# A hybrid scan-and-attention layer on one core: the low parts of the moving matrices placed 64 bytes further on

## What is computed

```python
h = adaLN(rmsnorm(x))                      # per-feature shift, scale, gate from SiLU(cond) @ w_ada
p = h @ w_in                               # q/k/v, r/k/v of the scan, low-rank codes, two branch gates
ya = rwkv_branch(...)                      # bidirectional scan with a 64x64 state per head
yb = neighbourhood_attention(...)          # 8 x 16 window of the grid, and the context tokens
x += gate1 * ((sig(gA) * (ya @ w_out_a) + sig(gB) * (yb @ w_out_b)) @ w_out)
x += gate2 * ((gelu(conv(h2 @ w_up_u)) * (h2 @ w_up_v)) @ w_ffn_down)   # h2 = adaLN(rmsnorm(x)), width 2816
```

## Time and profile before

| | |
|---|---|
| time, median of 3 runs | 2512.56 us (2512.36 to 2512.92) |
| the profiled execution's own time | 2510.91 us |
| its span, first to last instruction | 2509.1 us |
| mean granted TensorE clock | 0.983 |
| TensorE matmul busy | 2382.1 us, 95% |
| weight loads busy | 1964.0 us, 78% |
| VectorE, ScalarE, GpSimd busy | 1296.3, 725.6, 657.8 us |

### The profile page before, as it was taken

One profiled execution on the slowest core, in us unless ns is written; L12 is line 12 of the kernel. 1 busy time (PEld: TensorE's weight loads), 2 busy tenths in 40 slices (PEclk: granted clock), 3 DMA queues, 4 the chain that ended last, 5 costly groups with the idle time before them and its releaser, 6 DMA issues.

```text
span 2509.1 us, 50765 instructions
## 1 busy us (share of the span) xinstructions
PE 2382.1 (95%) x21658; PEld 1964.0 (78%) x21658; DVE 1296.3 (52%) x2077; ACT 725.6 (29%) x1189; POOL 657.8 (26%) x283
## 2 busy tenths in 40 slices
PE   5899999999999998889999998999999999999997
PEld 4777878788888887888745687888888888888886
DVE  4575657527568667895543323634333433443344
ACT  5273644634455553333300001201100110011002
POOL 2022020111211111222000244434344444444341
PEclk9999999999999999999989998999999999999999
DMA  6313111022266786676423310111111111111112
GB/s 281 109 35 106 55 60 62 28 95 76 93 193 193 202 230 191 196 204 183 154 75 115 119 35 26 34 34 43 35 42 34 43 34 43 34 42 37 40 34 93
DMA packets 224561, 234.53 MB, mean 93 GB/s; under 512 B 143922, under 2 KB 178866, under 8 KB 222898
## 3 DMA queue, kind: packets, MB, share of 16 engines
q1 hardware_dynamic: 199090, 229.55, 28.4%
q10 hardware_dynamic: 25344, 3.15, 0.8%
HBM read 173.80 MB, written 57.02 MB: 92 GB/s over the span
## 4 chain that ended last, share of the span: by engine, by line
PE 81%; DVE 8%; issue 3%; ACT 2%; DMA 2%; SPq 1%; ACTq 1%; POOL 1%; DVEq 0%; POOLq 0%
PE PS L878 20%; PE PS L879 20%; PE PS L880 20%; PE PS L1354 6%; PE PS L1022 3%; PE PS L994 2%; DVE buffer L2081 2%; PE PS L1008 1%; DVE buffer L2080 1%; PE PS L996 1%; DMA buffer<-in_w_ada_first 1%; ACTq L1729 1%; PE PS L1074 1%; PE PS L1164 1%; PE PS L1326 1%
## 5 line engine op out<-in xcount | busy, mean ns | idle before, releaser
L878 PE MATMUL PS<-buffer,buffer 128*128 128x512 f32 (+1 forms) x2784 | 997.5, 358 | 10.2 <-DVE buffer L1976 3.4
L879 PE MATMUL PS<-buffer,buffer 128*128 128x512 f32 (+1 forms) x2784 | 987.8, 355 | 1.7 <-issue 1.7
L880 PE MATMUL PS<-buffer,buffer 128*128 128x512 f32 (+1 forms) x2784 | 987.8, 355 | 0.0
L878 PEld LDWEIGHTS PS<-buffer,buffer 128*128 128x128 f32 x2784 | 525.6, 189 | 97.3 <-issue 17.0
L880 PEld LDWEIGHTS PS<-buffer,buffer 128*128 128x128 f32 x2784 | 525.6, 189 | 78.8 <-issue 2.1
L879 PEld LDWEIGHTS PS<-buffer,buffer 128*128 128x128 f32 x2784 | 525.9, 189 | 75.2 <-issue 1.0
L2366 POOL TENSOR_TENSOR buffer<-buffer,buffer 128x1024 fp32r<-128x1024 f32 x76 | 184.0, 2421 | 816.8 <-PE PS L880 510.4
L2309 DVE SCALAR_TENSOR_TENSOR buffer<-PS,buffer,buffer 128x512 f32<-128x512 f32 (+1 forms) x264 | 158.5, 655 | 151.4 <-PE PS L880 151.4
L2367 POOL TENSOR_TENSOR buffer<-buffer,buffer 128x1024 fp32r<-128x1024 f32 x76 | 194.1, 2554 | 6.0
L2285 DVE TENSOR_SCALAR buffer<-buffer,buffer 128x1281 f32<-128x1281 f32 x22 | 34.8, 1582 | 286.6 <-ACT buffer L1810 286.6
L1810 ACT ACTIVATE buffer<-PS 128x512 f32<-128x512 f32 (+1 forms) x66 | 30.0, 529 | 504.3 <-PE PS L880 504.3
(11 more groups left out here) (228 smaller groups left out, 2796.9 us busy)
## 6 DMA issues: line engine op xcount, KB each, us to landing
buffer<-in_w_up SPq DMA_DIRECT2D x44, 512.0 KB, 3.3
buffer<-in_w_in SPq DMA_DIRECT2D x42, 512.0 KB, 5.2
ops_kept<-buffer SPq DMA_DIRECT2D x40, 512.0 KB, 4.6
buffer<-ops_kept SPq DMA_DIRECT2D x80, 256.0 KB, 3.4
buffer<-in_w_ada SPq DMA_DIRECT2D x32, 512.0 KB, 6.3
buffer<-rkv_kept SPq DMA_DIRECT2D x120, 128.0 KB, 3.3
buffer<-in_w_down SPq DMA_DIRECT2D x22, 512.0 KB, 3.3
buffer<-in_x SPq DMA_DIRECT2D x20, 512.0 KB, 7.6
```

What stands on the lines that cost most here:

```text
L878: mm(out, w_hi, x_hi, start=start, stop=False)
L879: mm(out, w_hi, x_lo, start=False, stop=False)
L880: return mm(out, w_lo, x_hi, start=False, stop=stop)
```

## The change

`LO_SHIFT` of 16 words (64 bytes) is added to `LO_AT`, and so to all that is placed from it, and separately to the FFN's buffers behind `h2H`. No instruction is added, removed or moved on any engine; only addresses differ.

```diff
-        LO_AT = AFTER_YB + 12 * T
+        LO_SHIFT = 16
+        LO_AT = AFTER_YB + 12 * T + LO_SHIFT
@@
-        assert g3.at == LO_AT, (g3.at, LO_AT)
+        assert g3.at <= LO_AT, (g3.at, LO_AT)
@@
-        assert FREE + 3 * KB * T == LO_AT
+        assert FREE + 3 * KB * T <= LO_AT
@@
-        diag2 = view(FREE + 2 * KB * T, TB, P)
+        diag2 = view(FREE + 2 * KB * T + LO_SHIFT, TB, P)
@@
         h2H = view(FREE, KB, T, dtype=F32R)
-        h2_scaled_x = view(FREE + KB * T, KB, T)
-        h2L = view(FREE + KB * T, KB, T, dtype=F32R)
-        s5 = Space(FREE + 2 * KB * T)
+        h2_scaled_x = view(FREE + KB * T + LO_SHIFT, KB, T)
+        h2L = view(FREE + KB * T + LO_SHIFT, KB, T, dtype=F32R)
+        s5 = Space(FREE + 2 * KB * T + LO_SHIFT)
         factH = s5(3, T, dtype=F32R)
         factL = view(s5.at, 3, T, dtype=F32R)
```

## The result

The changed kernel takes 2532.96 us (median of 4 runs, 2530.02 to 2536.26) against 2512.46 for the kernel before: 1.0074 times as long, 95% interval 1.0056 to 1.0093. It is slower by some 20 us. The profiled execution is at 2530.02 us with a span of 2528.2, 19.1 us longer than before.

A forecast was written before the change was run, and what follows sets the result against it. The prediction took TensorE's matmuls, busy 95% of the span, to bound the kernel. Its terms summed to +0.1 us on 2510.9 profiled, 2512.6 by the median, predicted as 2512; own range 2508 to 2517, 8 in 10 range 2482 to 2537.

The forecast's parts named there:

- What bounds the kernel, and how to read it: Whole kernel: TensorE's matmuls, busy 95% of the span; only the distance between starts in an unbroken row counts.
- The sign of failure that I had named: Tiles and `ffn_up`: the forecast is wrong if distances between matmul starts change by over 1 ns on average.
- A matmul costs what its own pair of halves costs today: Split matmuls, stationary and moving operand: same half 227.2 ns wide, 119.6 narrow; different halves 229.0 and 116.4.
- `ffn_down`, which I put at -0.2 us: 528 triples of `ffn_down`: all three matmuls come to same halves; -1.9 us wide, +1.7 narrow, together -0.2.
- `tile` and `ffn_up`, -0.2: 1776 triples: only the second matmul's x moves, into its weights' half; -2.1 us wide, +1.9 narrow, together -0.2.
- the attention, 0.0: 288 triples of its projections: the first matmul gets different halves, the other two equal ones; 0.0 us.
- The bound for what I didn't know: Attention, tiles and `ffn_up`: 4128 switches of x's half, each up to 6.3 ns dearer or cheaper, +26 to -26 us; zero taken.
- The slow rival: Triples of attention, tiles and `ffn_up`: each of 4128 switches of halves costs up to 6.3 ns, +26 us, 2538.6; chance 0.26.
- The rival that nothing happens: Whole kernel: by the page's rules no placement in 64-byte steps costs anything; same time as forecast, within no change's 0.40.
- Nothing for the other engines: Moved buffers of VectorE, ScalarE and GpSimd: an engine of this kind pays nothing for the place.
- +0.5 us for `mix_block`: Plain float32 matmuls of `mix_block`: x leaves the half without their weights for theirs; 256 x 2 ns = +0.5 us.

The follow-up runs named there:

- down_only: Kernel before with only `factH` and `factL` (both together) and `x1` moved by 64 bytes; 1.0015 times the kernel before.
- ring_128_back: Kernel before with `WORDS` 32 less, so all weight tiles of the ring lie 128 bytes further back; 1.0071 times the kernel before.
- after_lo_back: Changed kernel with the ring's low weights moved 128 bytes against the high ones; 1.0037 times the kernel before, changed kernel 1.0083 on the same chip.

## Why the prediction was wrong

- **What bounds the kernel, and how to read it: right.** The sign of failure that I had named came: the distances in tiles and `ffn_up` grew by 2.6 and 3.2 ns wide. The loss is in the distance between starts in unbroken rows of split matmuls and nowhere else of size; that sum (+20.6 us) meets the measured 20.
- **"A matmul costs what its own pair of halves costs today": the step that failed.** From two placements in the trace, 0 and 192, I took a rule modulo 128. The runs show a period of 256 bytes with a sign: what I called "different halves" is 228.9 ns wide at +192 and 233.3 at +64, and "same halves" 226.9 at 0 and 232.4 at 128. So the terms had the wrong entry each time. `ffn_down`, which I put at -0.2 us as a return to the attention's state, came to a distance of 128 and cost +4.8; `tile` and `ffn_up`, -0.2, cost +12.9; the attention, 0.0, cost +3.0. Only in the attention, tiles and `ffn_up` are moving matrices mixed, and there no sum over single matmuls works either: in `ffn_up` the own distances modulo 256 give 230.1 ns of the table's 232.2, in the attention 229.0 of 233.3. The rest comes with the neighbours' operands.
- **The bound for what I didn't know: wide enough, and zero the wrong choice in it.** 4128 switches at up to 6.3 ns gave +26 us, and the wide range held that sum but for a little. So the measured 2533 us lies in it, though far outside the 2508 to 2517 of my forecast. In part that is luck: the stages that the bound was made for lost 15.9 us, and the other 4.8 are `ffn_down`'s, for which it had nothing. I chose the middle because two placements were equal within 0.2%; with an overhead that other placements move by 4 to 6 ns, equality of two of them says nothing about a third.
- **The slow rival: right in sign, near in price in part by luck, and no account of the loss.** down_only and ring_128_back lose without a switch, and after_lo_back keeps the switches and gets half of the loss back. That mixing the places of x costs something of its own is borne out, but not as a price for a switch of halves: it goes from +4.4 to -1.7 ns a matmul with the place of the weights.
- **The rival that nothing happens.** By the Trainium skill, page "SBUF — State Buffer", section "Specifications (TRN2)", the lines of SBUF have 16 bytes; taken alone, that would make every multiple of 64 bytes alike. The tables disagree for float32r: 226.9 to 233.3 ns. For bfloat16 and float32 they agree.
- **Nothing for the other engines: right. +0.5 us for `mix_block`: should have been zero.** VectorE's busy time rose by 1.6 us in 1296. The wide records of `mix_block` stand 429.2 ns apart before and after, and the run on types shows no effect of the distance on float32; the 2 ns were read from durations.

What stays open is the mechanism. It is tied to float32r, which alone here streams 4 bytes a column at a column a cycle, and to the place of both operands modulo 256; it grows with the length of the moving matrix and does not shrink with the width of the stationary one. Open too is what a mixed triple costs and what puts a row into one state or the other. That two streams of reads meet in the same part of the memory would fit the first half and was not shown.

## What to carry to other kernels

For float32r matmuls the place of the stationary against the moving matrix modulo 256 bytes is worth up to 3% of each matmul, so lay both out on purpose and measure: in the tables a distance of 0 is good for wide matmuls, 192 also, and nearly everything else is dear. In this layer there was nothing to gain by it: at 0 in place of 192 it took the same time, since the narrow matmuls and `ffn_down` lost what the wide ones gained. Read it from the distance of starts in the timeline, never from durations, and before deriving a rule from two placements make a table of them in a kernel of a few hundred microseconds. Where operands are bfloat16 or float32, leave their places alone.

## What the runs showed of the hardware

- The same instructions at the same addresses run in different states: 113.3 or 117.8 ns narrow, and at a distance of 16 bytes 226.7 or 233.3 wide. In the kernel before, such a state lasts through 16 weight tiles of `ffn_up` in a row, 1152 matmuls.
- At the lower clock the overhead is absent. In the kernel before, from 69.6 to 73.5 us, the granted clock is 0.50 of full speed, 1.2 GHz, and the narrow float32r matmuls stand 213.3 ns apart, which is 1.2 columns a ns; when it rises, the next ones stand 117 to 119 apart.
- The means over the column rate often lie at 6.7, 13.3 or 20.0 ns, which are 16, 32 and 48 cycles at 2.4 columns a ns. It is no rule: 117.8, 228.9 and 232.4 ns lie between them, and within one row the single distances of wide matmuls go from 228 to 241 (at a distance of 128), in a pattern that repeats after a few matmuls.
- With 128 columns on both sides, float32r matmuls stand 111.6 ns apart at every distance; with stationary matrices of 64 or 32 columns 60 to 62.
